# Attention stage of a hybrid decoder step: order of rotation, weight splits, high parts, sample items and output projection

## The reference

```python
def swa_qkv(h, pos, w_qkv, q_norm, k_norm):
    proj = h @ w_qkv                       # 1024 -> 16 query heads, 4 key heads, 4 value heads of 64
    ...
    q = rope_partial(rmsnorm(q, q_norm).astype(jnp.float32), pos).astype(h.dtype)
    k = rope_partial(rmsnorm(k, k_norm).astype(jnp.float32), pos).astype(h.dtype)
    return q, k, v

def swa_attend(q, k, v, mask, sinks):
    qg = q.reshape(q.shape[:-2] + (SWA_KV_HEADS, SWA_GROUP, SWA_HEAD_DIM))
    s = jnp.einsum('...qkgd,...skd->...kgqs', qg, k, preferred_element_type=jnp.float32) * (SWA_HEAD_DIM ** -0.5)
    s = jnp.where(mask[..., None, None, :, :], s, -jnp.inf)
    sink = sinks.astype(jnp.float32).reshape(SWA_KV_HEADS, SWA_GROUP, 1, 1)
    m = jnp.maximum(s.max(-1, keepdims=True), sink)
    p = jnp.exp(s - m)
    denom = p.sum(-1, keepdims=True) + jnp.exp(sink - m)
    o = jnp.einsum('...kgqs,...skd->...qkgd', (p / denom).astype(v.dtype), v)
    return o.reshape(q.shape)
```

## Time and profile before

| | us |
|---|---|
| median of the runs | 1344.32 |
| the profiled execution, its own time | 1343.74 |
| its span | 1342.0 |
| PE busy | 1288.3 (96%) |
| DVE busy | 702.7 (52%) |
| ACT busy | 508.1 (38%) |
| chain that ended last | PE 90%, DVE 6%, ACT 2% |
| the stage: last qkv units to the output projection | about 775 to 895 |

### The profile page before, as it was taken

The page is one execution under the profiler, slowest core; times in us unless marked ns, Lnnn a source line. Parts: engine busy times, 40 slices in busy tenths (PEclk is TensorE's granted clock), DMA queues, the critical chain, the costliest instruction groups (busy, mean ns, idle before and its releaser), DMA issues.

```text
span 1342.0 us, 25334 instructions
## 1 busy us (share of the span) xinstructions
PE 1288.3 (96%) x10091; PEld 966.8 (72%) x10091; DVE 702.7 (52%) x1120; ACT 508.1 (38%) x842; POOL 63.0 (5%) x205
## 2 busy tenths in 40 slices
PE   6999999999999999999999977889999999999998
PEld 6764577777777777777774435567777777777776
DVE  4633456466556566644433449835565666553322
ACT  4422245345333333333333455624433333332241
POOL 2000001000000000000020200000000000000000
PEclk9999999999999999999999978989999999999999
DMA  9422234223323332133253210003233332223341
GB/s 252 145 81 77 60 106 142 72 81 93 90 83 94 94 94 82 57 93 90 86 173 124 76 46 1 1 17 95 79 94 94 94 87 85 79 66 91 93 102 45
DMA packets 186819, 117.87 MB, mean 88 GB/s; under 512 B 5089, under 2 KB 177973, under 8 KB 186654
## 3 DMA queue, kind: packets, MB, share of 16 engines
q1 hardware_dynamic: 182058, 101.80, 26.0%
q0 software_dynamic: 4704, 15.26, 3.6%
HBM read 109.15 MB, written 9.86 MB: 89 GB/s over the span
## 4 chain that ended last, share of the span: by engine, by line
PE 90%; DVE 6%; ACT 2%; issue 1%; DMA 1%; SPq 0%; DVEq 0%; ACTq 0%
PE PS L302 72%; PE PS L1005 6%; PE PS L782 4%; ACT P L1331 1%; DVE st L1704 1%; PE PS L705 1%; DMA xtok<-in_x_prompt 1%; PE PS L873 1%; PE PS L893 1%; DVE ntmp L358 0%; PE PS L847 0%; ACT crow L525 0%; PE PS L876 0%; DVE P L1718 0%; PE PS L1110 0%
## 5 line engine op out<-in xcount | busy, mean ns | idle before, releaser
L274 DVE SCALAR_TENSOR_TENSOR wL<-stage,wH 128x1024 f16<-128x1024 f32 x204 | 248.9, 1221 | 257.3 <-ACT wH L268 257.3
L268 ACT ACTIVATE wH<-stage 128x1024 f16<-128x1024 f32 x204 | 214.3, 1051 | 284.2 <-PE PS L302 201.4
L302 PE MATMUL PS<-zL,wH 128*128 128x288 f16 x1408 | 287.8, 286 | 0.0
L302 PE MATMUL PS<-zH,wL 128*128 128x288 f16 x1408 | 287.8, 286 | 0.0
L302 PE MATMUL PS<-zH,wH 128*128 128x288 f16 x1408 | 287.8, 286 | 0.0
L302 PEld LDWEIGHTS PS<-zH,wH 128*128 128x128 f16 x1408 | 137.8, 98 | 35.0
L302 PEld LDWEIGHTS PS<-zH,wL 128*128 128x128 f16 x1408 | 137.8, 98 | 34.7
L302 PEld LDWEIGHTS PS<-zL,wH 128*128 128x128 f16 x1408 | 137.8, 98 | 34.7
L302 PE MATMUL PS<-hH,wH 128*128 128x288 f16 x704 | 143.8, 286 | 0.0
L302 PE MATMUL PS<-hL,wH 128*128 128x288 f16 x704 | 143.8, 286 | 0.0
L302 PE MATMUL PS<-hH,wL 128*128 128x288 f16 x704 | 143.8, 286 | 0.0
(11 more groups left out here) (326 smaller groups left out, 1553.9 us busy)
## 6 DMA issues: line engine op xcount, KB each, us to landing
stage<-in_w_ffn_up SPq DMA_DIRECT2D x88, 512.0 KB, 3.6
stage<-in_w_mlstm_in SPq DMA_DIRECT2D x24, 512.0 KB, 3.7
stage<-in_w_ffn_down SPq DMA_DIRECT2D x32, 384.0 KB, 3.0
stage<-in_w_ffn_down SPq DMA_DIRECT2D x32, 320.0 KB, 2.9
stage<-in_w_swa_qkv SPq DMA_DIRECT2D x12, 512.0 KB, 3.5
C<-in_state_mlstm_C POOLq DMA_DIRECT2D x4, 1024.0 KB, 6.0
stage<-in_w_mlstm_out SPq DMA_DIRECT2D x8, 512.0 KB, 3.4
out_sample_C<-C POOLq DMA_DIRECT2D x4, 1024.0 KB, 5.1
```

What stands on the lines that cost most here:

```text
L268: nc.scalar.activation(wH[:, slot, :], stage[:, slot, :], ACT.Copy, scale=WSCALE).then_inc(hi_ready, 1)
L274: nc.vector.scalar_tensor_tensor(out=wL[:, slot, :], in0=stage[:, slot, :], scalar=WSCALE, in1=wH[:, slot, :], op0=ALU.mult, op1=ALU.subtr ...
L302: m = nc.tensor.matmul(out[:, hf, :], w[a][:, slot, 128 * (at + j):128 * (at + j + 1)], xs(b, k)[:, HALF * hf:HALF * (hf + 1)], start=(fir ...
```

## The change

- Chunk 2 of the qkv projection: all steps left of norm_rope(1) are taken ahead of the splits on DVE; on ACT `rms` comes ahead of the first split of a chunk. The split of unit 3 of this chunk (for unit 3 of the output projection) is moved on both engines to item 10 (`LATE_SPLIT`).
- At the end of chunk 2 ACT only squares, and DVE copies out, each tile behind its square.
- scores(0) and scores(1) stand ahead of groups 12 and 13 on PE, exps(0) ahead of their copies on ACT, maxima(0) and (1) ahead of norm_rope(2).
- Both banks of the turned probabilities are copied by ACT in one instruction (one bank for n=0); DVE's copies go. `ptA` and `ptV` become `pt`.
- ACT does `out_high(x-1)` of a prompt item ahead of `exps(x+2)`.
- The two sample items become items 12 and 13, ahead of the last four of the prompt; they have rows of `st` of their own, now 4 deep. `scaled(x-1)` moves ahead of `normalise(x+1)`, and `back` follows the scores two items on.
- `first_half(0)` and `first_half(1)`: tiles k 0 to 3 of the first two units of the output projection, behind values(15) and values(16). The rest of these units follows the last item, and units 2 to 7 are written out instead of looped.

```diff
@@
-        ITEMS = [(n, J, hp) for J in range(2) for n in range(4) for hp in range(2)] + [(-1, s, 0) for s in range(2)]
+        ITEMS = [(n, J, hp) for J in range(2) for n in range(4) for hp in range(2)]
+        ITEMS[12:12] = [(-1, s, 0) for s in range(2)]
@@
+        def st_of(x):
+            return x % 2 if ITEMS[x][0] >= 0 else 2 + ITEMS[x][1]
+
+        LATE_SPLIT = 10
@@ PE
             def turn(x):
                 n, J, hp = ITEMS[x]
                 if n >= 0:
-                    pe.wait_ge(asem["p"], x + 1)
+                    pe.wait_ge(asem["p"], sum(i >= 0 for i, _, _ in ITEMS[:x + 1]))
                 else:
                     pe.wait_ge(asem["e"], x + 1)
                 if x:
-                    if ACT_PT[x - 1]:
-                        pe.wait_ge(asem["ptA"], ACT_PT[x - 1])
-                    pe.wait_ge(asem["ptV"], x)
+                    pe.wait_ge(asem["pt"], x)
@@ PE
+            def first_half(u):
+
+                pe.wait_ge(asem["e"], NI - 1 + u)
+                pe.wait_ge(asem["ol"], NI - 4)
+                fm_unit(pe, unit("sout", 0, u), range(4), normed, pair(u), True, False, done=False)
@@ PE
             scores(0)
             scores(1)
+            for g in BEFORE_UNIT[4]:
+                group(g)
             for x in range(NI):
                 if x in BESIDE_ITEM:
                     group(BESIDE_ITEM[x])
                 if x + 2 < NI:
                     scores(x + 2)
+                if x >= 2 and ITEMS[x - 2][0] < 0:
+                    back(ITEMS[x - 2][1])
                 turn(x)
                 if x:
                     values(x - 1)
-                    if x == NI - 1:
-                        back(0)
+                if x >= NI - 2:
+                    first_half(x - NI + 2)
             values(NI - 1)
-            back(1)
             pe.wait_ge(asem["ol"], NI)
-            pe_fm_seg(pe, "sout", None)
+            for u in range(2):
+                fm_unit(pe, unit("sout", 0, u), range(4, KD), normed, pair(u), False, True, at=4)
+            for t in range(2, 8):
+                pe.wait_ge(res["sout"][0], t + 1)
+                fm_unit(pe, unit("sout", t // 4, t % 4), range(KD), normed, pair(t % 4), True, True)
@@ ACT
+                    if c and u == 0:
+                        rms(c - 1)
                     split_act(act, ahead(unit("qkv", c, u)))
                     if c == 0 and u == 0:
                         column_rstd()
-                    if c and u == 0:
-                        rms(c - 1)
@@ ACT
-                if n != 0:
-                    if x >= 2:
-                        act.wait_ge(asem["o"], x - 1)
-                    nc.scalar.activation(PT[:, x % 2, 0, :], PS[:, 4, :], ACT.Copy).then_inc(asem["ptA"], 1)
+                if x >= 2:
+                    act.wait_ge(asem["o"], x - 1)
+                if n == 0:
+                    nc.scalar.activation(PT[:, x % 2, 1, :], PS[:, 5, :], ACT.Copy).then_inc(asem["pt"], 1)
+                else:
+                    nc.scalar.activation(PT[:, x % 2, :, :], PS[:, 4:6, :], ACT.Copy).then_inc(asem["pt"], 1)
+                if x and ITEMS[x - 1][0] >= 0:
+                    out_high(x - 1)
                 if x + 2 < NI:
                     exps(x + 2)
-                if x:
+                if x and ITEMS[x - 1][0] < 0:
                     out_high(x - 1)
@@ DVE
             for c in range(3):
                 next(steps, None)
-                for u in range(4):
+                if c == 2:
+                    for _ in steps:
+                        pass
+                for u in range(3 if c == 2 else 4):
                     split_dve(dve, ahead(unit("qkv", c, u)))
                     next(steps, None)
+                if c == 2:
+                    for tt in range(TT):
+                        dve.wait_ge(asem["sq"], tt + 1)
+                        src, dst = by_key_head(PS[0:ROWS[tt], tt, :], qtok[0:ROWS[tt], tt, 512:1024])
+                        nc.vector.tensor_scalar(dst, src, rcol[0:ROWS[tt], tt:tt + 1], None,
+                                                ALU.mult).then_inc(free["qkv"], 1)
@@ DVE
             for x in range(NI):
-                n, J, hp = ITEMS[x]
+                if x == LATE_SPLIT:
+                    split_dve(dve, ahead(unit("qkv", 2, 3)))
                 if x + 2 < NI:
                     maxima(x + 2)
-                rows = 128 if n >= 0 else NS
-                dve.wait_ge(asem["t"], x + 1)
-                if x >= 2:
-                    dve.wait_ge(asem["o"], x - 1)
-                nc.vector.tensor_copy(PT[0:rows, x % 2, 1, :], PS[0:rows, 5, :]).then_inc(asem["ptV"], 1)
+                if x and ITEMS[x - 1][0] < 0:
+                    scaled(x - 1)
                 if x + 1 < NI:
                     normalise(x + 1)
                 if x:
```

More of the change, by code:

```diff
@@ L238, in build @@
         c_out = [sem("c_outa"), sem("c_outb")]
-        asem = {s: sem("attn_" + s) for s in ("rss", "rs", "rope", "tr", "trA", "trV", "s", "m", "e", "p", "t",
-                                              "ptA", "ptV", "o", "os", "ob", "oh", "ol", "cz", "kz")}
+        asem = {s: sem("attn_" + s) for s in ("sq", "rss", "rs", "rope", "tr", "trA", "trV", "s", "m", "e", "p", "t",
+                                              "pt", "o", "os", "ob", "oh", "ol", "cz", "kz")}
         dKV = sem("dKV")
@@ L672, in group_evac, with by_key_head @@
             m.then_inc(asem["trA"], 1)
+        def st_of(x):
+            return x % 2 if ITEMS[x][0] >= 0 else 2 + ITEMS[x][1]
+        LATE_SPLIT = 10
+        def by_key_head(src, dst):
+            return (src.rearrange("p (a g d) -> p a g d", a=2, d=HD), dst.rearrange("p (g a d) -> p a g d", a=2, d=HD))
         def score_banks(x):
@@ L1015, in _ @@
                         column_sums()
-            for g in BEFORE_UNIT[4]:
-                group(g)
             pe.wait_ge(masks_in, 1)
@@ L1307, in _ @@
                     src, dst = PS[0:r, tt, :], qtok[0:r, tt, 512 * QKV[c]:512 * (QKV[c] + 1)]
-                    nc.scalar.activation(sqx(tt)[0:r, 0:normed_cols], src[:, 0:normed_cols], ACT.Square,
-                                         scale=rcol[0:r, tt:tt + 1])
+                    m = nc.scalar.activation(sqx(tt)[0:r, 0:normed_cols], src[:, 0:normed_cols], ACT.Square,
+                                             scale=rcol[0:r, tt:tt + 1])
+                    if c == 2:
+                        m.then_inc(asem["sq"], 1)
+                        continue
                     if c:
-                        src = src.rearrange("p (a g d) -> p a g d", a=2, d=HD)
-                        dst = dst.rearrange("p (g a d) -> p a g d", a=2, d=HD)
+                        src, dst = by_key_head(src, dst)
                     nc.scalar.activation(dst, src, ACT.Copy, scale=rcol[0:r, tt:tt + 1]).then_inc(free["qkv"], 1)
-                split_act(act, ahead(unit("qkv", c, 3)))
-            for g in BEFORE_UNIT[4]:
-                group_evac(act, g)
+                if c < 2:
+                    split_act(act, ahead(unit("qkv", c, 3)))
             def exps(x):
@@ L1343, in _ @@
             exps(0)
+            for g in BEFORE_UNIT[4]:
+                group_evac(act, g)
+            exps(1)
             rms(2)
-            exps(1)
             for x in range(NI):
@@ L1348, in _ @@
                     group_evac(act, BESIDE_ITEM[x])
+                if x == LATE_SPLIT:
+                    split_act(act, ahead(unit("qkv", 2, 3)))
                 n, J, hp = ITEMS[x]
                 act.wait_ge(asem["t"], x + 1)
-                if n != 0:
-                    if x >= 2:
-                        act.wait_ge(asem["o"], x - 1)
-                    nc.scalar.activation(PT[:, x % 2, 0, :], PS[:, 4, :], ACT.Copy).then_inc(asem["ptA"], 1)
+                if x >= 2:
[6 more added lines that the diff above has]
+                    out_high(x - 1)
                 if x + 2 < NI:
                     exps(x + 2)
-                if x:
+                if x and ITEMS[x - 1][0] < 0:
                     out_high(x - 1)
@@ L1690, in maxima @@
                 dve.wait_ge(asem["s"], x + 1)
-                s = st[:, x % 2]
+                s = st[:, st_of(x)]
                 b0 = score_banks(x)
@@ L1727, in scaled @@
                 nc.vector.tensor_tensor(osb[:, :, :], PS[:, 6, 0:256].rearrange("p (i d) -> p i d", i=4),
-                                        st[:, x % 2, 1, :].unsqueeze(2).to_broadcast([128, 4, HD]),
+                                        st[:, st_of(x), 1, :].unsqueeze(2).to_broadcast([128, 4, HD]),
                                         ALU.mult).then_inc(asem["os"], 1)
             def out_low(x):
-                if ITEMS[x][0] < 0:
-                    scaled(x)
                 dve.wait_ge(asem["oh"], x + 1)
@@ L1738, in _ @@
             maxima(0)
+            maxima(1)
             next(steps, None)
-            maxima(1)
             normalise(0)
             for x in range(NI):
```

(10 more changed lines are left out.)

10 lines of the change are left out of this document (4 added, 6 removed).

## The result

| | before | after |
|---|---|---|
| median of the runs, us | 1344.78 (1343.53 to 1345.42, 4 runs) | 1326.11 (1323.20 to 1326.89, 4 runs) |
| the profiled execution | 1343.74 | 1325.73 |
| PE busy | 1288.3 (96%) | 1281.3 (97%) |
| DVE busy | 702.7 x1120 | 695.4 x1107 |
| ACT busy | 508.1 x842 | 513.4 x841 |

The ratio is 0.9859, with an interval of 0.9843 to 0.9874: 1.4% faster. The forecast was 1322.9, the range 1316 to 1332. The direction and the place are right; the median is 3.2 above the forecast, and 0.1 above the 1319 to 1326 that the forecast was given by itself.

A forecast was written before the change was run, and what follows sets the result against it. TensorE was taken as the bound, weak only in the attention stage, where it waits and loses clock. Gains 7.7 + 7.8 + 8.2 = 23.7, less 1.0 and 1.3, gave 21.4: 1322.3 profiled, 1322.9 median; range 1316 to 1332.

The forecast's parts named there:

- Ahead of T0: Up to the last qkv unit's end (T0): rotation ahead of the splits ends PE's wait, 7.7 us gained.
- Start of the rounds: Just behind the last qkv unit's end (T0): maxima(0) starts at T0+1.45 instead of T0+3.48, 2.0 us sooner.
- rounds 0 to 4: First attention rounds: DVE sets the pace, turn(4) at T0+26.4; 5.2 us gained, including 2.0 from the start.
- Full rounds: Attention rounds with the loop cut: a full round falls from 4.32 to 3.65 us, bound by PE.
- The sign that I gave: Full attention rounds: 3.65 with PE nearly full, and the low part's wait for the high part gone.
- Turn(11): End of the rounds: turn(11) at T0+54.0, 7.8 us gained up to here; the moved splits cost 1.9.
- rival 2: Turn(4) to round 6: clock does not recover when PE is the bound, costs 8 us: 1331; chance 0.12.
- The sign of being wrong: Attention stage: scaled() waits over 2 us each, ACT's copy over 1.2, or clock under 0.9 behind T0+30.
- Drain: Turn(11) to the output projection's remaining matmuls: 33.8 us, 5.9 of it projection done early; 8.2 us gained.
- Sum: Whole stage: 23.7 us gained, less 1.0 for semaphore hops and 1.3 for clock, 21.4 net.
- Rival 3: At 776.7, ahead of the last qkv unit: another late releaser, 5 to 7 us lost: 1328; chance 0.06.
- Rival 4: PE-bound 56 us of work: PE granted half clock there, all of it gives 1378, slower; chance 0.02.

The follow-up runs named there:

- rot_alone: Kernel before the change with only the rotation moved: norm_rope(1) steps ahead of chunk 2's splits, rms ahead of a chunk's first split; 1336.96 us, ratio 0.9938.
- no_rot: Changed kernel with the steps of norm_rope(1) spread between the splits of chunk 2 again; 1332.19 us.
- high_late: Changed kernel with every high part behind the exponentials again on ACT; 1328.20 us.
- two_copies: Changed kernel with the turned probabilities copied by ACT and DVE again, one bank each; 1330.61 us.
- split_17: Changed kernel with LATE_SPLIT at item 17 instead of 10; 1320.73 us, ratio 0.9813.
- fill: Changed kernel with 6, 13 and 8 matmuls that nobody reads ahead of turn(0), turn(2) and turn(4); 1322.71 us, ratio 0.9831.
- half_ahead: Changed kernel with the late split at item 17 and the first half unit ahead of turn(16); 1318.58 us, ratio 0.9793.
- no_half: Changed kernel without the two half units, all eight output projection units done behind the last item; 1324.64 us.
- after_again: The changed kernel measured once more, nothing altered; 1327.48 us, ratio 0.9859.

## Why the prediction was right, and where it was off

- **Ahead of T0**: forecast 7.7, measured 8.0, and shown alone and taken back. That all steps of the rotation are done long ahead of their reader held (7.5 us of cover). What the term missed is that by rot_alone 1.1 and by no_rot 1.6 of it is lost again behind turn(4) by the clock; in the changed kernel this is the same 1.6 as under turn(11) below. I had summed stages as if the clock in one did not depend on what PE did in the one before.
- **Start of the rounds and rounds 0 to 4**: T0+1.49 and T0+26.5, against 1.45 and 26.4. Adding up DVE's instructions, tried on the kernel before first, was good to 0.1.
- **Full rounds**: 3.65, PE-bound, as forecast; taking back either edit costs 5.4 (high_late) and 5.5 (two_copies). The sign that I gave, no more wait of the low part for the high part, did not come true as written: DVE still has such waits, from 0.20 to 0.83 behind turn(4) and longer ones at the end. As PE is the bound there they cost nothing, but for the last, behind which PE waits its 0.94. In rounds 0 to 3 they are gone.
- **Turn(11)**: off by 1.8. The cost of the moved splits was sized right (1.9 forecast, 2.0 in split_17). The times from T0 left the clock out; the sum allowed 1.3 for it in the whole stage, from one gap of before. Half clock behind turn(4) alone cost 1.6, which fill gave back, and the gap ahead of turn(2) cost nothing. Of rival 2, half clock from turn(4) through round 6, only the start came true: it lasted some 4 us, with 1.00 from 820 on. The sign of being wrong, under 0.9 behind T0+30, was touched for 1 us (0.57 in 817 to 818). The other two were not: the waits in scaled() are 1.40 and 0.74, ACT's copy takes 1.02.
- **Drain**: from turn(11) to the rest of L302 34.0, forecast 33.8. The first half unit stands 24.0 behind turn(11); the forecast's T0+76.7 is 22.7 behind it, but the drain's own terms add up to 23.8, so this was a slip in adding and not in a term. The gap ahead of turn(16), forecast 1.85, is 1.89, and the last wait 0.94 for 1.0. Of the gain, 3.2 is the samples' place, which also keeps the clock up for L302, and 1.3 the half units. I had not split the 8.2 so.
- **Sum**: the stage gave 22.0 against 23.7 raw and 21.4 net. Of the 2.3 taken off, the clock took 1.6 where I had 1.3. The 1.0 for semaphore hops is shown by no run: turn(4) was 0.1 late, the drain 0.2 longer, and the gain up to T0 0.3 larger, so hardly anything of it was there. That the net is off by only 0.6 is thus in part luck. What failed is the step that carried it to the whole: I took all else in the profiled execution as unchanged, and the start was 3.7 later. 1343.74 - 22.0 + 3.7 + 0.25 gives 1325.7, the profiled time. A range of a few us for the start was not in my working. Kernels with the changed order start at 41.2 to 46.1, so a lasting cost is not shown, nor excluded: the mean over the twelve is about 44.5, against 42.1 and 41.6 in the two with the order of before.
- **Rival 3** (another late releaser) did not occur: no wait at L982. **Rival 4** (half clock through the PE-bound stretch) neither: 1.00 in nearly all of it.

## What to carry to other kernels

Cut a stage at points that are seen in both traces, add up each engine's instructions between them, and try that sum on the kernel before; it found a loop of 4.32 and its replacement of 3.65 exactly. Where two engines wait for each other in turn, look first at the order: one short instruction of 0.3 moved ahead of a long one was worth 5.4 us here. And work belongs on the engine with room in that stretch, even if it takes longer there. Wherever TensorE waits for some 2 us, look for work of its own to put ahead of the wait, as the half unit here: it fills the gap and spares the half clock that may come behind it, together 3.3 us between split_17 and half_ahead.

## What was not expected of the hardware

- **A gap of the same length is followed by half clock in one kernel and not in another.** Ahead of turn(16), after has a gap of 1.89 and the matmuls behind it take 1.09, full clock; split_17 has 1.88 there and they take 1.97 and 1.82. The only edit between the two is the place of one split, which moved the gap by some 2 us. Not even that is needed: no_half does the same as after up to turn(16), with the same gap of 1.96 ahead of turn(11), and lost 1.6 behind it where after lost nothing. So the price of a gap was 0 to 1.6 here, and cannot be told from its length alone; and a difference of 1.6 in S between two kernels, each with one profile, need not come from the edit. The Trainium skill (TensorE: Matmul & The Clock Gate, Part 1: The HAM clock gate) says of the start of a kernel that the count of slow matmuls varies from run to run. Here it is a place in mid-kernel, and between after and after_again it did not vary: S is the same to the hundredth.
- **Matmuls whose result nobody reads kept the clock at 1.00** in two stretches where it was 0.74 and 0.71, and were worth 1.6 us for no PE time that mattered: turn(2) and turn(4) stand where they stood. All three kernels that have them kept it; of the other kernels with the new order, no_rot and high_late had 1.00 behind turn(4) without them.
- **The time to the first projection matmul differs by 4.9 us** (41.2 to 46.1) between executions of programs with the same start, part late load and part half clock behind the wait for it, as much as several of the edits tried here are worth. Edits of 2 us were told apart by S and the turn times, not by the medians.
